# A two-layer hybrid decoder in one program: x's first tile on ScalarE's queue, and the score products of two differential heads issued as one block

## The chip, the cores and the metric

The kernel runs on one core of a Trainium2 chip. The metric is the device time of one execution in microseconds, the median of several runs. Five engines work side by side, each on a list of instructions of its own that it takes strictly in order: TensorE (PE in the profile), VectorE (DVE), ScalarE (ACT), GpSimd (POOL) and SyncE (SP, which here only starts DMAs). They wait for one another through semaphores.

## The reference

All of it is f32, with 256 tokens, a model width of 1024 and two layers. Cut to what matters here:

```python
for l in range(DEPTH):                                    # DEPTH = 2
    h = rms_norm(x, norm_mix[l])
    qkv = (h @ w_in[l]).reshape(B, S, 3, 16, 64)          # w_in: 1024 x 3072
    # heads 0..3: differential attention, two softmaxes of 32 dimensions each
    s1, s2 = q1 @ k1.T * scale, q2 @ k2.T * scale         # causal
    o_a = (softmax(s1) - lam * softmax(s2)) @ v
    # heads 4..9: three dilated windows mixed; heads 10..15: block-sparse, here plain causal
    x = x + concat(o_a, o_b, o_c) @ w_out[l]
    x = x + memory_cross_attention(rms_norm(x, norm_cross[l]), rms_norm(mem, norm_mem[l]), ...)
    x = x + (silu(g) * u) @ w_down[l]                     # g, u = rms_norm(x, norm_ffn[l]) @ w_gate_up[l]
```

## The kernel before

**Split products.** Every weight tile of 128 x 2048 numbers (a *unit*, 1 MB, loaded by SP into one of three ring slots `raw`, `whi`, `wlo`) is rounded by ACT (`split_hi`, line 591 or 583) into `whi`, and DVE (`split_lo`, line 886) writes the rest into `wlo`. PE then makes hi·hi, hi·lo and lo·hi. A slot is loaded again when both splits of the unit in it are done. x is treated in the same way: PE transposes a quarter of x (`build_x`, line 1394), ACT writes `thi` (`x_hi`, line 603), DVE `tlo` (`x_lo`, line 946).

**The sequence g.** The first stage of each layer is written by hand as steps g = 0, 1, 2, ... PE does one *filler* per step, four matmuls 128x512 of the q/k/v projection (line 1457, six steps to a unit, twelve to a chunk of 512 columns). Tables at the foot of the file say at which g the other work stands between the fillers, and ACT and DVE go through the same g in their own lists:

- `CHAIN_AT[e]`: DVE's norm of the k heads with its rotary (e = 0, 2) or of the q heads (e = 1, 3; the rotary of q is then POOL's, lines 534 to 537). `QKT_AT[e]`: PE's transposes of those heads (line 1548), and ACT's and DVE's copies of them to `kT`, `qT`.
- `S_AT[d]`: PE's `score(d)` (line 1587): the products of softmaxes 2d and 2d+1 with two query tiles, each f32 matmul standing in the trace as two records. There are 20 softmaxes: 0 to 7 are the eight of the four differential heads (32 rows of the array each), the rest have 64 rows. At the same g DVE does `mask_max` for both softmaxes (line 1117), which reads PSUM and writes `prob`. ACT's exponentials (`exps`, line 679) stand one and two steps later, and DVE's `combine` (lines 1126 to 1131: p1 - lam*p2 of a differential head) four steps later.
- `T_AT[m]`: PE transposes head m's probabilities (line 1599). `V_AT[m]`: PE's product with v (lines 1622 to 1624).
- DVE has, besides, `reduce_squares` (line 1024) at g = 12i + 13, and `split_lo` of unit g//6 + 2 at every g with g % 6 = 1. ACT has `split_hi` of that unit at g % 6 = 0, the copies of finished chunks (line 647) and the squares (line 657).

Two score blocks share two PSUM banks, so `score(d)` waits until DVE has read the block before (`nmax`). `mask_max` waits, where a `prob` buffer is used again, until PE has transposed the old one. The six tiny DVE steps of `lambdas` (line 984) run once, in layer 0.

## Time and profile before

| | us |
|---|---|
| median of 3 runs | 723.79 |
| lowest and highest of them | 720.84, 726.49 |
| the profiled execution | 718.44 |
| its span, first to last instruction | 716.6 |
| PE busy in the span | 693.4 |
| DVE busy | 474.6 |
| ACT busy | 396.7 |
| POOL busy | 128.4 |

The profile is of one execution, and its span lies 1.8 us below that execution's own time. The profile's page gives busy times, a chain of waits followed back from the end, and groups of instructions; the trace behind it gives each stretch in order of time, with a note in brackets where an engine sat idle and what released it. A row of the timeline merges neighbours: "x8" is eight records, and the duration is from the first's start to the last's end. Since neighbours overlap, the distance between two starts is the better price of a step.

### The profile page before, as it was taken

The numbers are of one execution on the slowest core, as the hardware profiler recorded it, in microseconds if no ns is written. First come the engines' busy times: TensorE is split into PE (matmuls) and PEld (weight loads), VectorE is DVE, ScalarE is ACT, GpSimd is POOL, SyncE is SP. The second block draws the span as 40 slices with busy tenths as digits, with TensorE's granted clock in tenths as the row PEclk, the third lists the DMA queues.
The fourth block names the chain that finished last, engine by engine and source line by source line (L and its number), as shares of the span: only waits on it lengthen the run. The fifth ranks groups of instructions, "written<-read, shape, count | busy, mean of one in ns | idle before, by whom it ended". The sixth has DMA issues, their size and how long they took to land.

```text
span 716.6 us, 10788 instructions
## 1 busy us (share of the span) xinstructions
PE 693.4 (97%) x3820; PEld 584.1 (82%) x3820; DVE 474.6 (66%) x935; ACT 396.7 (55%) x645; POOL 128.4 (18%) x100
## 2 busy tenths in 40 slices
PE   6999999999999999999999999999899999999997
PEld 4877788878988888888878878888688888888886
DVE  3899944374866666666569897344566666666665
ACT  5965767376644444444466658764765444444442
POOL 7131027507000000000031210662440000000000
PEclk9999999998999999999999999999999999999999
DMA  9945422244466666556545635022455566666631
GB/s 305 316 137 175 142 95 89 89 117 145 147 180 180 198 198 184 176 176 176 183 169 179 234 116 177 17 102 71 111 175 174 176 181 201 204 202 194 188 117 59
DMA packets 121215, 115.64 MB, mean 161 GB/s; under 512 B 3008, under 2 KB 95312, under 8 KB 121184
## 3 DMA queue, kind: packets, MB, share of 16 engines
q1 hardware_dynamic: 120224, 113.32, 50.8%
q0 software_dynamic: 384, 1.14, 0.6%
q10 hardware_dynamic: 576, 0.77, 0.3%
q8 instruction: 18, 0.29, 0.2%
q14 instruction: 13, 0.11, 0.0%
HBM read 114.17 MB, written 1.05 MB: 161 GB/s over the span
## 4 chain that ended last, share of the span: by engine, by line
PE 83%; DVE 11%; ACT 4%; issue 1%; DMA 1%; POOL 0%; SPq 0%; ACTq 0%; DVEq 0%
PE ps L1813 20%; PE ps L1457 16%; PE ps L1818 11%; PE ps L1850 5%; PE ps L1851 5%; PE ps L1852 5%; PE ps L1526 3%; DVE wlo L886 3%; PE ps L1835 3%; PE ps L1420 2%; PE ps L1587 2%; PE ps L1781 2%; PE ps L1394 2%; PE ps L1599 1%; ACT whi L591 1%; PE ps L1623 1%
## 5 line engine op out<-in xcount | busy, mean ns | idle before, releaser
L886 DVE TENSOR_TENSOR wlo<-raw,whi 128x2048 fp32r<-128x2048 f32 (+1 forms) x89 | 197.7, 2240 | 37.3 <-ACT whi L591 36.1
L591 ACT ACTIVATE whi<-raw 128x2048 fp32r<-128x2048 f32 (+1 forms) x103 | 191.0, 1878 | 14.3 <-PE ps L1852 7.3
L1813 PE MATMUL ps<-both,whi 128*128 128x512 f32 x640 | 159.2, 391 | 0.0
L1813 PEld LDWEIGHTS ps<-both,whi 128*128 128x128 f32 x640 | 117.6, 188 | 22.7
L1457 PE MATMUL ps<-whi,both 128*128 128x512 f32 x384 | 101.8, 401 | 2.7 <-ACT whi L583 2.0
L486 POOL TENSOR_TENSOR wlo<-raw,whi 128x2048 fp32r<-128x2048 f32 x15 | 68.5, 4581 | 196.3 <-DVE xs L975 180.8
L834 ACT ACTIVATE qkv<-ps 128x512 f32<-128x512 f32 x44 | 26.4, 599 | 126.9 <-PE ps L1818 121.7
L1818 PEld LDWEIGHTS ps<-both,wlo 128*128 128x128 f32 x640 | 87.3, 190 | 6.2
L1818 PE MATMUL ps<-both,wlo 128*128 128x256 f32 x640 | 89.2, 282 | 0.0
L1457 PEld LDWEIGHTS ps<-whi,both 128*128 128x128 f32 x384 | 71.4, 190 | 19.3 <-ACT both L603 2.4
L1850 PE MATMUL ps<-whi,ahi 128*128 128x512 f32 x176 | 69.3, 394 | 1.6 <-DVE alo L1353 1.6
L1851 PE MATMUL ps<-wlo,ahi 128*128 128x512 f32 x176 | 69.0, 392 | 0.0
L1852 PE MATMUL ps<-whi,alo 128*128 128x512 f32 x176 | 68.5, 389 | 0.0
L1332 DVE TENSOR_TENSOR qkv<-ps,qkv 128x512 f32<-128x512 f32 x44 | 30.3, 688 | 52.5 <-ACT qkv L834 52.4
L1457 PE MATMUL ps<-wlo,both 128*128 128x512 f32 x192 | 53.6, 401 | 0.1
L842 ACT ACTIVATE qkv<-qkv 128x256 f32<-128x256 f32 x44 | 18.4, 418 | 57.7 <-DVE qkv L1337 57.7
L679 ACT ACTIVATE sq<-sq,nm 128x128 f32<-128x128 f32 x80 | 35.4, 448 | 15.7 <-DVE nm L1117 15.5
L1457 PEld LDWEIGHTS ps<-wlo,both 128*128 128x128 f32 x192 | 34.7, 188 | 10.3 <-issue 3.3
L946 DVE SCALAR_TENSOR_TENSOR both<-ps,g_rows,both 128x128 fp32r<-128x128 f32 x96 | 25.9, 343 | 22.9 <-ACT both L603 22.9
L1850 PEld LDWEIGHTS ps<-whi,ahi 128*128 128x128 f32 x176 | 33.2, 189 | 8.2 <-DVE alo L1353 2.5
L1852 PEld LDWEIGHTS ps<-whi,alo 128*128 128x128 f32 x176 | 33.1, 188 | 7.2
L1851 PEld LDWEIGHTS ps<-wlo,ahi 128*128 128x128 f32 x176 | 33.2, 189 | 5.2
(202 smaller groups left out, 923.8 us busy)
## 6 DMA issues: line engine op xcount, KB each, us to landing
raw<-in_w_gate_up SPq DMA_DIRECT2D x88, 512.0 KB, 5.1
raw<-in_w_in SPq DMA_DIRECT2D x23, 1024.0 KB, 5.2
raw<-in_w_down SPq DMA_DIRECT2D x22, 1024.0 KB, 4.9
raw<-in_w_out SPq DMA_DIRECT2D x8, 1024.0 KB, 5.0
raw<-in_w_mkv SPq DMA_DIRECT2D x4, 1024.0 KB, 5.3
raw<-in_w_mq SPq DMA_DIRECT2D x4, 512.0 KB, 3.6
raw<-in_w_mo SPq DMA_DIRECT2D x2, 1024.0 KB, 4.9
xs<-in_x SPq DMA_DIRECT2D x2, 512.0 KB, 5.6
```

Source lines behind the costliest of these rows:

```text
L486: pool.tensor_tensor(wlo[s][:, 0:n], raw[s][:, 0:n], whi[s][:, 0:n].bitcast(F32), ALU.subtract)\
L591: ins = act.activation(whi[s][:, cols], raw[s][:, cols], ACT.Copy)
L679: ins = act.activation(prob[n % 4][:, a:b], prob[n % 4][:, a:b], ACT.Exp, bias=nm[:, n, t:t + 1], scale=-1.0, accum_out=zs[:, n, t:t + 1])
L834: act.activation(small_gu[b], gu_banks(b, 1), ACT.Copy).then_inc(small_out.sem, 1)
L886: ins = dve.tensor_tensor(wlo[s][:, cols], raw[s][:, cols], hi, ALU.subtract)
L1332: dve.tensor_tensor(gu[b], gu_banks(b, 0), small_gu[b], ALU.add).then_inc(gu_done.sem, 1)
L1457: ins = pe.matmul(ps[:, acc, :], x_part[:, k0 + k, t * P:(t + 1) * P], w_part[s][:, 512 * k:512 * k + 512], start=first and k == 0 and par ...
L1813: pe.matmul(ps[:, bank, :], whi[s][:, a:a + P], both[:, :, k, :], start=(k == 0), stop=False)
L1818: ins = pe.matmul(ps[:, bank, 0:256], wlo[s][:, a:a + P], thi[:, k, :], start=False, stop=(k == KC - 1))
L1850: pe.matmul(acc, ahi[b][:, tok], whi[s][:, a:a + 512], start=first, stop=False)
L1851: pe.matmul(acc, ahi[b][:, tok], wlo[s][:, a:a + 512], start=False, stop=False)
L1852: ins = pe.matmul(acc, alo[b][:, tok], whi[s][:, a:a + 512], start=False, stop=last)
```

## The change

Its parts, in the order of the diff:

1. **Start.** x's first tile is loaded by ACT's queue, ahead of its two small constants, and no longer stands between the identity and the first weights on SP's queue. The first unit's four pieces are rounded half by DVE (0 and 1) and half by ACT (2 and 3); ACT does its two between the first and the second quarter of x, and DVE takes `wlo` piece by piece. PE runs eight dummy products of a tile of ones ahead of everything and three after the first transposes (`WARM`).
2. **Score block.** The scores of heads 0 and 1 are issued as one block at g = 45 and those of heads 2 and 3 at g = 55. The four softmaxes stand in row groups 0, 32, 64 and 96 and write four banks (0, 1, 3, 4) where two banks served before. DVE does its four `mask_max` together. ACT's exponentials of the second head stand two steps behind the first's.
3. **Waits.** Banks 3 and 4 also serve `transpose_qk(2)` and the first products with v, so these now wait until all eight differential softmaxes are masked (`nmax` 8).
4. **Tables.** The positions of nearly all steps of the stage move.

```diff
             sp.dma_start(ident, consts["ident"]).then_inc(s_ident.sem, 16)
-            sp.dma_start(xs[:, 0, :], x_in[:, 0, :]).then_inc(s_x[0].sem, 16)
...
+            x_in = x.rearrange("b (t p) d -> p (b t) d", p=P)
+            act.dma_start(xs[:, 0, :], x_in[:, 0, :]).then_inc(s_x[0].sem, 16)
             act.dma_start(g_rows[:].rearrange("p l g k -> p (l g k)"), consts["g_rows"]).then_inc(s_rows.sem, 16)
             act.dma_start(freqs[:], consts["freqs"]).then_inc(s_freq.sem, 16)
...
-                    for k in range(4):
+                    for k in (2, 3):
                         cols = slice(512 * k, 512 * k + 512)
                         act.wait_ge(s_first[k].sem, 16)
                         ins = act.activation(whi[s][:, cols], raw[s][:, cols], ACT.Copy)
...
-                        split_hi(0, 0)
                         squares_of_x(0, 0, 0)
                     for q in (2 * t, 2 * t + 1):
                         x_hi(layer, X_MIX, q)
+                        if layer == q == 0:
+                            split_hi(0, 0)
...
-                            if g == S_AT[d] + b + 1:
+                            if g == exp_at(d) + b + 1:
                                 exps(2 * d + b)
...
                 if layer == 0:
-                    for q in range(2):
-                        x_lo(layer, X_MIX, q)
-                    split_lo(0, 0)
+                    for k in range(2):
+                        cols = slice(512 * k, 512 * k + 512)
+                        dve.wait_ge(s_first[k].sem, 16)
+                        dve.tensor_copy(whi[0][:, cols], raw[0][:, cols]).then_inc(first_hi_dve.sem, 1)
+                    x_lo(layer, X_MIX, 0)
+                    for k in range(4):
+                        cols = slice(512 * k, 512 * k + 512)
+                        if k < 2:
+                            dve.wait_ge(first_hi_dve.sem, k + 1)
+                        elif k == 2:
+                            dve.wait_ge(first_hi.sem, 1)
+                        else:
+                            dve.wait_ge(hi_done[0].sem, 1)
+                        ins = dve.tensor_tensor(wlo[0][:, cols], raw[0][:, cols], whi[0][:, cols].bitcast(F32), ALU.subtract)
+                    ins.then_inc(lo_done[0].sem, 1)
+                    x_lo(layer, X_MIX, 1)
...
-                        ins = dve.tensor_tensor_reduce(prob[n % 4][:, a:b], ps[:, n % 2, a:b], masks[:, kind, a:b],
+                        ins = dve.tensor_tensor_reduce(prob[n % 4][:, a:b], ps[:, score_bank(n), a:b], masks[:, kind, a:b],
...
-                        if d < DIFF and g == S_AT[d] + 4:
+                        if d < DIFF and g == exp_at(d) + 4:
                             combine(d)
...
+            def warm_up(n):
+
+                for _ in range(n):
+                    pe.matmul(ps[:, 7, 0:P], ones[:], ones[:], start=True, stop=True)
+
+            pe.wait_ge(s_ones.sem, 1)
+            warm_up(WARM[0])
             pe.wait_ge(s_ident.sem, 16)
             for layer in range(DEPTH):
 
                 for q in range(2):
                     build_x(layer, X_MIX, q)
+                if layer == 0:
+                    warm_up(WARM[1])
 
...
                     for b in range(2):
+                        if e == 2 and b == 0:
+                            pe.wait_ge(nmax.sem, nmax.at(layer, 4 if QKT_AT[2] < S_AT[2] else 2 * DIFF))
                         if e == 3 and b == 0:
...
                 def score(d):
 
-                    if d:
+                    together = (d, d + 1) if d < DIFF else (d,)
+                    if d == 2:
+
+                        pe.wait_ge(nmax.sem, nmax.at(layer, 4))
+                        pe.wait_ge(qkT_act.sem, qkT_act.at(layer, 3 if QKT_AT[2] < S_AT[2] else 2))
+                        pe.wait_ge(qkT_dve.sem, qkT_dve.at(layer, 3 if QKT_AT[2] < S_AT[2] else 2))
+                    elif d:
                         pe.wait_ge(nmax.sem, nmax.at(layer, 2 * d))
                     for qa, qb, kb, a in ((0, P, P, 0), (P, 2 * P, 2 * P, P)):
-                        for n in (2 * d, 2 * d + 1):
+                        for n in range(2 * d, 2 * d + 2 * len(together)):
                             h, base, rows = SOFTMAXES[n]
                             q, k = qT[base:base + rows, h // 2, qa:qb], kT[base:base + rows, h // 2, 0:kb]
-                            ins = pe.matmul(ps[:, n % 2, a:a + kb], q, k, start=True, stop=True)
-                    ins.then_inc(scores.sem, 1)
+                            ins = pe.matmul(ps[:, score_bank(n), a:a + kb], q, k, start=True, stop=True)
+                            if a and n % 2:
+                                ins.then_inc(scores.sem, 1)
 
                 def transpose_p(m):
                     n = 2 * m if m < DIFF else m + DIFF
...
                     if m == 0:
 
+                        pe.wait_ge(nmax.sem, nmax.at(layer, 2 * DIFF))
...
-                    for d in range(DUOS):
+                    for d in (0, 2) + tuple(range(DIFF, DUOS)):
                         if g == S_AT[d]:
...
+WARM = (8, 3)
 QK_CHUNKS = (0, 1, 2, 3)
 
 
-CHAIN_AT = (14, 26, 46, 53)
-QKT_AT = (30, 43, 56, 72)
-S_AT = (45, 49, 55, 61, 67, 70, 73, 78, 83, 86)
-T_AT = (54, 57, 64, 69, 71, 72, 76, 77, 78, 79, 82, 83, 87, 88, 91, 92)
-V_AT = (64, 67, 69, 71, 77, 77, 78, 79, 82, 82, 86, 88, 91, 92, 95, 95)
+CHAIN_AT = (17, 31, 54, 60)
+QKT_AT = (32, 42, 60, 72)
+S_AT = (45, 45, 55, 55, 67, 70, 73, 78, 83, 86)
+T_AT = (52, 54, 64, 66, 71, 72, 73, 77, 78, 79, 82, 83, 87, 88, 91, 92)
+V_AT = (64, 67, 71, 73, 77, 77, 78, 79, 82, 82, 86, 88, 91, 92, 95, 95)
 V_CHUNKS = (4, 5)
 SUMS = [(0, 0, 0), (0, 0, 1), (1, 0, 0), (1, 0, 1), (1, 1, 0), (2, 0, 0), (2, 0, 1), (2, 1, 0)]
-SUB_AT = 75
+SUB_AT = 76
 MEM_AT = (19, 20, 21, 22)
-MEM_SQ_AT = 22
+MEM_SQ_AT = 21
 HB_AT = (81, 82, 91)
-KM_AT = 89
+KM_AT = 86
 N_BUILD = 3
-LAM_AT = 13
-MEM_ROOT_AT = 41
+LAM_AT = 7
+MEM_ROOT_AT = 42
 LAST = max(FILLERS + 3 * len(OUT1_EARLY) - 1, V_AT[-1])
 
 
...
+def exp_at(d):
+
+    return S_AT[d] + (2 * (d % 2) if d < DIFF else 0)
+
+
+def score_bank(n):
+
+    return (0, 1, 3, 4)[n % 4] if n < 2 * DIFF else n % 2
 
```

What the tables make of the lists, at the three places that matter most. PE in layer 0, before, from the first score block (line 1587, `kT` and `qT`) to the first transposes of probabilities (line 1599, `sq` holds `prob`):

```order
L1587 MATMUL ps<-kT,qT 128x128 x2
L1587 MATMUL ps<-kT,qT 128x256 x2
L1457 MATMUL ps<-whi,both 128x512 x4
L1457 MATMUL ps<-wlo,both 128x512 x4
L1457 MATMUL ps<-whi,both 128x512 x8
L1587 MATMUL ps<-kT,qT 128x128 x2
L1587 MATMUL ps<-kT,qT 128x256 x2
L1457 MATMUL ps<-wlo,both 128x512 x4
L1457 MATMUL ps<-whi,both 128x512 x8
L1457 MATMUL ps<-wlo,both 128x512 x4
L1457 MATMUL ps<-whi,both 128x512 x4
L1599 MATMUL ps<-ident_sb,sq 128x128 x3
```

Of the change (its lines are numbered higher: 1622 is the score block, 1635 the transposes of probabilities, 1577 those of the k heads), from the first transposes of probabilities on:

```order
L1635 MATMUL ps<-ident_sb,sq 128x128 x3
L1484 MATMUL ps<-wlo,both 128x512 x4
L1484 MATMUL ps<-whi,both 128x512 x4
L1635 MATMUL ps<-ident_sb,sq 128x128 x3
L1484 MATMUL ps<-whi,both 128x512 x4
L1622 MATMUL ps<-kT,qT 128x128 x4
L1622 MATMUL ps<-kT,qT 128x256 x4
L1484 MATMUL ps<-wlo,both 128x512 x4
L1484 MATMUL ps<-whi,both 128x512 x8
L1484 MATMUL ps<-wlo,both 128x512 x4
L1484 MATMUL ps<-whi,both 128x512 x4
L1577 MATMUL ps<-ident_sb,qkv 128x128 x8
```

The second head's probabilities are transposed two fillers behind the first's, the block of heads 2 and 3 follows one filler later, and the transposes of the k heads of the second half come five fillers after that; four blocks have become two.

DVE in the same stretch, before: the first two masks (line 1117), then the norm of the second half of k (from line 918 to 1085), then `combine(0)` (1126), two masks, `reduce_squares`, `split_lo` of unit 10 (886) and `combine(1)`.

```order
L1117 ISA nm 128x1
L918 TENSOR_SCALAR nv<-g 128x16
...
L1085 TENSOR_TENSOR qkv<-rope_dve 128x2x6x8
L1126 RECIPROCAL lam_z<-zs 128x2
...
L1131 SCALAR_TENSOR_TENSOR sq<-sq,lam_z 128x256
L1117 ISA sq,nm<-ps,table,q_root 128x128
...
L1024 TENSOR_REDUCE g<-sqc 128x2x8
L886 TENSOR_TENSOR wlo<-raw,whi 128x2048
L1126 RECIPROCAL lam_z<-zs 128x2
```

DVE now, from the last of the first four masks (line 1133) on: 1142 to 1147 is `combine`, 1040 the reduction, 889 `split_lo`, 921 to 1101 the norm of k.

```order
L1133 ISA nm 128x1
L1142 RECIPROCAL lam_z<-zs 128x2
...
L1147 SCALAR_TENSOR_TENSOR sq<-sq,lam_z 128x256
L1040 TENSOR_REDUCE g<-sqc 128x2x8
L889 TENSOR_TENSOR wlo<-raw,whi 128x2048
L1142 RECIPROCAL lam_z<-zs 128x2
...
L1147 SCALAR_TENSOR_TENSOR sq<-sq,lam_z 128x256
L921 TENSOR_SCALAR nv<-g 128x16
...
L1101 TENSOR_TENSOR qkv<-rope_dve 128x2x6x8
L1133 ISA sq,nm<-ps,table,q_root 128x128
```

Both combines and a `split_lo` now stand ahead of the norm of k, and four masks stand right behind it, ahead of everything that PE takes from DVE next.

ACT in the same stretch, before, from the last exponential (679) of softmax 1 on: a finished chunk (647), the squares (657), `split_hi` of unit 10 (591, slot 1), and only then softmax 2:

```order
L679 ACTIVATE sq,zs<-sq,nm 128x256
L647 ACTIVATE qkv<-ps,rs 128x512
L657 ACTIVATE sqc<-qkv 128x1024
L591 ACTIVATE whi1<-raw1 128x2048
L679 ACTIVATE sq,zs<-sq,nm 128x128
```

And now, from the finished chunk (650) on; 682 is softmax 2's exponential, in two parts, 660 the squares, 593 `split_hi`:

```order
L650 ACTIVATE qkv<-ps,rs 128x512
L682 ACTIVATE sq,zs<-sq,nm 128x128
L682 ACTIVATE sq,zs<-sq,nm 128x256
L660 ACTIVATE sqc<-qkv 128x1024
L593 ACTIVATE whi1<-raw1 128x2048
```

Softmax 2 has moved ahead of the squares and of that `split_hi`; softmax 3 still comes behind them.

## Rows read from the trace of the kernel before

**Rows 1.** The page's first part: busy us, share of the span, instructions.

```profile
PE 693.4 (97%) x3820; PEld 584.1 (82%) x3820; DVE 474.6 (66%) x935; ACT 396.7 (55%) x645; POOL 128.4 (18%) x100
```

**Rows 2.** Chain of waits over the first 60 us, summed by line.

```profile
by line: DVE wlo L886 25.9%; PE ps L1457 6.9%; ACT both L603 6.8%; ACT whi L591 6.0%; DMA xs<-in_x 6.0%; DVE g L1024 5.8%; DVE mlo L953 4.1%; issue 3.6%; PE ps L1394 3.3%; ACT L754 2.1%; ACT qkv L647 2.1%; ACT sqc L657 1.8%; ACT sq L618 1.3
```

**Rows 3.** Timeline of PE at the start: start, duration, instruction, idle before.

```profile
4.91 1.94 PE L1394 MATMUL ps<-ident_sb,xs 128*128 128x128 f32 x8 [4.91 <-DMA xs<-in_x]
...
8.87 4.13 PE L1457 MATMUL ps<-whi,both 128*128 128x512 f32 x8 [2.02 <-ACT whi L583]
```

**Rows 4.** Timeline of ACT and DVE around 28 us, layer 0.

```profile
27.12 1.90 ACT L591 ACTIVATE whi<-raw 128x2048 fp32r<-128x2048 f32 x1
27.25 1.22 DVE L1024 TENSOR_REDUCE g<-sqc 128x32 f32<-128x1024 f32 x1 [1.94 <-ACT sqc L657]
...
29.84 2.26 DVE L886 TENSOR_TENSOR wlo<-raw,whi 128x2048 fp32r<-128x2048 f32 x1
```

**Rows 5.** Timeline of DVE from the first masks on, layer 0.

```profile
59.74 0.34 DVE L1117 CUSTOM_DVE_ANT_0 sq<-ps,table,q_root 128x128 f32<-128x128 f32 x1
...
67.61 0.16 DVE L1126 RECIPROCAL lam_z<-zs 128x2 f32<-128x2 f32 x1
...
70.08 1.22 DVE L1024 TENSOR_REDUCE g<-sqc 128x16 f32<-128x1024 f32 x1
71.22 2.28 DVE L886 TENSOR_TENSOR wlo<-raw,whi 128x2048 fp32r<-128x2048 f32 x1
...
74.53 0.16 DVE L1039 TENSOR_SCALAR nv<-g 128x4 f32<-128x4 f32 x1
...
77.38 0.34 DVE L1117 CUSTOM_DVE_ANT_0 sq<-ps,table,q_root 128x128 f32<-128x128 f32 x1
...
81.60 0.16 DVE L1126 RECIPROCAL lam_z<-zs 128x2 f32<-128x2 f32 x1
```

**Rows 6.** Timeline of PE from the first score block on, layer 0.

```profile
58.66 0.92 PE L1587 MATMUL ps<-kT,qT 32*128 32x128 f32 x8
59.52 1.21 PE L1457 MATMUL ps<-whi,both 128*128 128x512 f32 x4
...
67.16 1.07 PE L1457 MATMUL ps<-wlo,both 128*128 128x512 f32 x4
...
68.98 0.49 PE L1599 MATMUL ps<-ident_sb,sq 128*128 128x128 f32 x3
69.22 1.17 PE L1457 MATMUL ps<-whi,both 128*128 128x512 f32 x4
...
74.67 0.55 PE L1599 MATMUL ps<-ident_sb,sq 128*128 128x128 f32 x3 [0.49 <-DVE sq L1131]
...
86.33 0.33 PE L1622 MATMUL ps<-qkv,probT 128*128 128x64 f32 x2
...
87.03 0.93 PE L1587 MATMUL ps<-kT,qT 64*128 64x128 f32 x8
```

**Rows 7.** Timeline of ACT after the first masks, layer 0.

```profile
60.53 0.40 ACT L679 ACTIVATE sq<-sq,nm 128x128 f32<-128x128 f32 x1 [1.07 <-DVE nm L1117]
...
62.61 0.69 ACT L647 ACTIVATE qkv<-ps,rs 128x512 f32<-128x512 f32 x1 [0.22 <-PE ps L1457]
...
64.30 1.90 ACT L591 ACTIVATE whi<-raw 128x2048 fp32r<-128x2048 f32 x1
```

**Rows 8.** Timeline of ACT and DVE ahead of layer 1's first masks.

```profile
408.02 0.58 ACT L665 ACTIVATE qT<-ps 128x512 f32<-128x512 f32 x1
...
410.73 0.34 DVE L1117 CUSTOM_DVE_ANT_0 sq<-ps,table,q_root 128x128 f32<-128x128 f32 x1
```

**Rows 9.** Timeline of POOL, the rotary of q, layer 0.

```profile
50.27 2.62 POOL L535 TENSOR_TENSOR rope_pool<-qkv,tab 128x128 f32<-128x128 f32 x1
```

**Rows 10.** Stretches: length, busy us (records) of each engine, PE clock, DMA.

```profile
155.00:162.00 7.00, 5.19 (x34) 3.53 (x34) 5.88 (x19) 4.52 (x13) 2.01 (x2) 0.91 0.34 83
162.00:170.00 8.00, 7.67 (x47) 7.27 (x45) 2.86 (x8) 6.33 (x12) 7.72 (x2) 0.65 0.22 66
```

More of the change, by code:

```diff
@@ L218, in trunk @@
         first_hi = signal("first_hi")
+        first_hi_dve = signal("first_hi_on_dve")
         s_first = [signal(f"first_weight_loaded{k}") for k in range(4)]
@@ L1452, in piece @@
                     for k in range(4):
-                        if first_piece and k < 3:
-                            pe.wait_ge(first_hi.sem, k + 1)
+                        if first_piece and k < 2:
+                            pe.wait_ge(first_hi_dve.sem, k + 1)
+                        elif first_piece and k == 2:
+                            pe.wait_ge(first_hi.sem, 1)
                         elif first_piece:
@@ L1857, in _ @@
                 gate_up(0, 0)
-                if layer == 0:
-                    pe.wait_ge(s_ones.sem, 1)
                 pe.wait_ge(diag_ready.sem, diag_ready.at(layer, 1))
```

## The prediction

> **What bounds the kernel now.** I read the page first: PE works 693.4 us of a span of 716.6 us [rows 1], so as a whole the program is bound by PE, and a gain has to shorten PE's list or fill one of its few gaps. The chain of waits over the first 60 us says something else about the stage that this change touches: its largest share, 25.9%, is DVE's `split_lo`, and PE's filler line has 6.9% [rows 2]. PE is busy there too, but it runs just behind DVE. DVE's timeline shows it: from 29.84 us [rows 4] to the first masks at 59.74 us and on to 81.6 us [rows 5] DVE's blocks follow one another nearly without a gap. And PE's timeline has the mark of it: at 74.67 us it has sat idle for 0.49 us for `combine(1)` [rows 6]. So I price the attention stage on DVE's list, and PE's only as the partner that may have to wait.
>
> **Prices.** Each is a distance between starts, in layer 0.
> - Filler: (68.98 - 67.16)/2 = 0.91 us. A transposition of probabilities: 0.24 us, and 0.1 us more on the filler behind it, 0.34 [rows 6].
> - Score block before: 59.52 - 58.66 = 0.86 us, and its next filler takes 0.14 more (1.21 against 1.07), so 1.0 us [rows 6].
> - One product with v: 87.03 - 86.33 = 0.70 [rows 6].
> - DVE: `combine` plus two masks is 70.08 - 67.61 = 2.47. Two masks plus the norm of k are 67.61 - 59.74 = 7.87. `reduce_squares` is 71.22 - 70.08 = 1.14. `split_lo` plus `combine` are 74.53 - 71.22 = 3.31, with `split_lo` at 2.20 (its 2.28 less the overlap), so `combine` is 1.11, two masks 1.36, the norm of k 6.51. The norm of q is 77.38 - 74.53 = 2.85. From 77.38 to 81.60 stand two masks, `split_lo` and the copy to `kT`: the copy is 0.66 [rows 5].
> - ACT: the first exponential starts 0.79 after the first mask. Two softmaxes take 62.61 - 0.22 - 60.53 = 1.86, so 0.93 each; chunk and squares 64.30 - 62.61 = 1.69; `split_hi` 1.90 [rows 7].
>
> **The score block.** Nothing in the trace has four row groups at work at once. If the four stand side by side, the joint block costs the old 1.0 us; if they only take turns in pairs, 2.0. The change removes two of four blocks in each layer, so PE's list gets shorter by between 0 and 4.0 us in both layers together. I take 4.0, since the old block puts eight records into 0.92 us [rows 6], which leaves no time for them one after another. [...] As the next parts show, this list is not what decides.
>
> **The start.** Now PE waits 4.91 us for x, and its first eight matmuls take 4.13 us [rows 3] where two groups of four take 1.82 later [rows 6]. Earlier work on PE and `whi` shared between two engines can give back at most that difference, some 2.3 us, and nothing at the least, since x now shares the DMA engines with the weights. I expect 1.3. But by 28 us DVE's and ACT's lists set the pace, and what they make of it counts. The lambda block, 29.84 - 27.25 - 1.14 = 1.45 us, moves to g = 7, into the 1.94 us in which DVE idles there [rows 4]. `split_lo` behind it cannot start at once: its `whi` is ready at 27.12 + 1.90 = 29.0 [rows 4], and ACT's list ahead of it gets a little longer in wait, so I place it at 29.4 for 29.84, 0.44 earlier. `lambda_ends` moves ahead too, some 0.4. So the first masks of layer 0 come about 0.9 us earlier than 59.74, at 58.9. The bounds are 0 and 1.9.
>
> **The first masks of layer 1.** There `split_hi` of unit 9 stood ahead of `qkT_out(1)` in ACT's list, and stands behind it now, both at g = 42. `qT` is copied at 408.02 [rows 8], now 0.91 earlier, and ends by 407.7. `whi` is ready at 409.6, `split_lo` takes 2.2, and the masks start at 411.8 for 410.73 [rows 8]: 1.1 us later, unless ACT has room elsewhere (bounds 0 and 1.5).
>
> **From the first masks to score block 4.** Call the start of the first mask M. Before, block 4 starts at 87.03 - 59.74 = M + 27.3 [rows 5, 6]. DVE's new list, in its order:
> - four masks to M + 2.7, `combine(0)` to 3.8;
> - the reduction needs ACT's squares. ACT does exponentials 0 and 1 to M + 2.65, the chunk to 3.4, exponential 2 to 4.3, squares to 5.25, `split_hi` 10 to 7.15, exponential 3 to 8.1. So the reduction runs 5.25 to 6.4;
> - `split_lo` 10 waits for its `whi`: 7.15 to 9.35. `combine(1)` to 10.45;
> - norm of k to 17.0, four masks to 19.7.
>
> PE reaches the transposition of head 1 with its scores, nine fillers and one transposition: 1.0 to 0.2 before M, plus 8.2 + 0.34, so M + 7.5 to 8.4. It waits for `combine(1)`, 2 to 3 us. From there it needs 0.34 + 0.91 + 1.0 + 4.55 = 6.8 to the transposes of k, M + 17.2. They wait for the rotary (17.0, there in time) and, new, for all eight masks: 19.7. A second wait of 2.5 us. This wait does not depend on the price of the block.
>
> Then DVE: `split_lo` 2.20, `combine(2)` 1.11, copy 0.66, norm of q 2.85, `combine(3)` 1.11, to M + 27.6. PE gets to head 3's transposition with 0.9 for the transposes of k, six fillers 5.46, 0.70 and 0.34, at M + 27.1: a third wait of 0.5. Behind it 0.24 + 1.0 + 0.70, and block 4 starts at M + 29.5. That is 2.2 later than before; 0.34 of it is head 3's transposition, which used to come later, so 1.9 per layer. What stands behind has slack: DVE waited for PE there.
>
> **The sum.** Layer 0: -0.9 + 1.9 = +1.0. Layer 1: +1.1 + 1.9 = +3.0. In all +4.0 us. The profiled execution of 718.44 becomes 722.4. The median of the runs shown, 723.79, lies 5.35 above that execution, and the same step on it gives 727.8 us, 0.6% more. The saved blocks (4.0 us of PE's list) and the start are in this sum, but PE spends them on waits: 5 to 6 us in each layer where it had 0.49.
>
> **Rivals.**
> - *The change does what it says, and PE stays the bound.* 4.0 from the blocks, 1.0 from the two old waits of 0.49, 2.0 from the start: 7.0 less, 716.8. For it: PE has 97% of the span. Against it: from `combine(1)` to the transposes of k DVE alone needs 6.51 + 2.72 = 9.2 us and PE 6.8, at prices that each stand in a row. It would need DVE to start that stretch 2.5 us ahead of PE. Something between this and the forecast (half of the waits) gives about 722. Chance 0.17, and 0.12 for the middle.
> - *POOL's rotary is caught.* In layer 0, `split_lo` of unit 7 now stands ahead of the norm of q, which then ends near 51.0, and POOL's four operations follow. One of them took 2.62 us [rows 9] while a `split_lo` ran beside it. If the last is caught by the next `split_lo`, the transposes of q wait 2.3 us and M moves by as much: 730.1. Against it: a reduction and a copy stand between, about 1.8 us. [...] Chance 0.10.
> - *The clock falls (slower).* [...] The two waits above leave PE idle for 5 of some 17 us. [...] Against it: around the old wait of 0.49 us the stage kept its full clock. Chance 0.13.
> - The forecast itself: 0.48.
>
> **How the numbers follow.** About 1%, 7 us, can be told from no change. Faster by more needs 716.5 or less: half of the first rival, 0.08. Slower by more needs 731.0: the clock, and a little of POOL's case, 0.14. Within 1%: 0.78. The forecast's own bounds are M's: 727.8 - 2.0 and 727.8 + 1.4. The range reaches to the first rival and towards the last, 717.5 to 731.5; outside lie most of the clock's case and a part of the first rival's, 0.2.
>
> **What would show it.** In the profile after: PE idle for `combine` at the second head's transposition, 2 to 3 us, and for the last mask at the transposes of the second half of k, about 2.5 us, in both layers; a score block of eight softmax products at 1.0 us; first masks near 58.9 and, counted from the layer's first filler, 1.1 later in layer 1; PE's idle time up by some 8 us. The forecast is wrong if those waits are under 1 us, if M comes 2 us earlier than said (then PE finds DVE ahead), or if the score block costs 2 us. If PE's clock is below 1.0 between 60 and 90 us, the last rival has come.

## The result, and the profile after

The changed kernel takes 723.6 us (median), the kernel before 719.7 us in the runs beside it: a ratio of 1.0046, 95% interval 1.0023 to 1.0068. By that ratio it is 3.3 us slower (the two medians lie 3.9 apart), within 1%. The 723.79 us that the prediction starts from was the median of three runs; the 719.7 is that of twenty. The profiled executions have spans of 721.0 and 716.6 us, 4.4 apart. Part 1 of the page after, and the chain's line:

```profile
PE 695.6 (96%) x3842; PEld 586.2 (81%) x3842; DVE 479.4 (66%) x940; ACT 395.7 (55%) x643; POOL 128.7 (18%) x100
...
PE 78%; DVE 12%; ACT 5%; POOL 2%; issue 2%; DMA 1%; ACTq 0%; DVEq 0%; POOLq 0%
```

PE is busy for 2.2 us more than in [rows 1], with two score blocks fewer in each layer. In part that is the eleven dummy products (22 records more), in part a fallen clock, which the next rows show. PE's timeline after, layer 0 (L1622 is the score block, L1635 the transposition of probabilities, L1577 that of k, L1484 the filler):

```profile
58.82 0.94 PE L1622 MATMUL ps<-kT,qT 32*128 32x128 f32 x16
...
67.47 1.08 PE L1484 MATMUL ps<-whi,both 128*128 128x512 f32 x4
71.51 0.79 PE L1635 MATMUL ps<-ident_sb,sq 128*128 128x128 f32 x3 [2.95 <-DVE sq L1147]
71.94 2.05 PE L1484 MATMUL ps<-whi,both 128*128 128x512 f32 x4
73.93 1.47 PE L1622 MATMUL ps<-kT,qT 32*128 32x128 f32 x16
...
80.04 1.03 PE L1577 MATMUL ps<-ident_sb,qkv 128*128 128x128 f32 x8
...
87.83 0.55 PE L1635 MATMUL ps<-ident_sb,sq 128*128 128x128 f32 x3 [0.28 <-DVE sq L1147]
...
89.85 0.93 PE L1622 MATMUL ps<-kT,qT 64*128 64x128 f32 x8
```

The sixteen records of the joint block (eight products) now take 0.94 us, as the eight of an old block did (0.92, [rows 6]). But the wait for `combine(1)` is 2.95 us for 0.49, and behind it a filler takes 2.05 for 1.08: the clock has fallen. The second wait of the forecast, 2.5 us at the transposes of k, is not there at all. The stretches of after (length, busy us of PE, PEld, DVE, ACT, POOL, then PE's granted clock, DMA share, GB/s):

```profile
60.00:67.00 7.00, 7.00 (x33) 5.73 (x32) 5.74 (x22) 5.14 (x15) 0.80 (x2) 1.00 0.77 252
67.00:72.00 5.00, 2.05 (x11) 1.44 (x9) 4.28 (x10) 2.17 (x6) 1.11 (x3) 0.97 0.02 7
72.00:76.00 4.00, 4.00 (x25) 2.59 (x24) 3.52 (x15) 2.29 (x2) 0.00 (x0) 0.61 0.71 254
76.00:90.00 14.00, 13.72 (x75) 11.32 (x75) 13.45 (x49) 10.03 (x28) 1.24 (x4) 1.00 0.24 77
150.00:180.00 30.00, 25.98 (x180) 21.99 (x179) 18.21 (x47) 20.64 (x52) 15.66 (x5) 1.00 0.50 141
```

PE was busy for 2.05 of 5 us, then the granted clock was 0.61 on the mean for 4 us (0.50 in each microsecond from 72 to 75), then 1.00 again. Layer 1 has the same behind its wait of 2.27 us (0.57 from 423 to 427 us, 0.50 from 424 to 426). At 160 us, where the clock had fallen before [rows 10], it stayed full.

DVE's timeline after, layer 0, M being the first mask:

```profile
61.06 0.34 DVE L1133 CUSTOM_DVE_ANT_0 sq<-ps,table,q_root 128x128 f32<-128x128 f32 x1
...
66.16 1.22 DVE L1040 TENSOR_REDUCE g<-sqc 128x16 f32<-128x1024 f32 x1 [1.19 <-ACT sqc L660]
67.96 2.38 DVE L889 TENSOR_TENSOR wlo<-raw,whi 128x2048 fp32r<-128x2048 f32 x1 [0.59 <-ACT whi L593]
...
71.37 0.17 DVE L921 TENSOR_SCALAR nv<-g 128x16 f32<-128x16 f32 x1
...
76.80 0.35 DVE L1133 CUSTOM_DVE_ANT_0 sq<-ps,table,q_root 128x128 f32<-128x128 f32 x1
```

M is 61.06, not 58.9. From there the list runs much as forecast: reduction at M + 5.1 (5.25), `split_lo` at M + 6.9 (7.15), norm of k at M + 10.3 (10.45), second masks at M + 15.7 (17.0). In brackets are the forecast's places.

**Where the 4.4 us are.** Both traces are cut at three points: PE's transposes of x for the cross attention of layer 0 (143.10 before, 145.63 after), those that open layer 1 (363.75, 364.80), and those for its cross attention (494.06, 496.85). The four pieces differ by +2.53, -1.48, +1.74 and +1.61. The first splits at M: +1.32 ahead of it, +1.21 behind. The third too: +0.50 and +1.24. The second and the fourth hold no changed work. They differ, as far as the windows show, by where the clock fell: at 160 us only before, in the fourth piece only after (a mean of 0.94 from 520 to 550 us). A second profile of the kernel before (e8 below), with full clock in both, has 219.2 and 222.6 us for them, where before has 220.7 and 222.5 and after 219.2 and 224.2. The two nearly cancel.

### The profile page after: what moved, and what is told of

Read it like the earlier page. It is cut to its first block, busy times and chain, and to the rows that moved or that the text cites. A ratio compares the mean times of both kernels' runs of the same rounds, so it can differ in the third digit from the quotient of the medians.

```text
span 721.0 us, 10838 instructions
## 1 busy us (share of the span) xinstructions
PE 695.6 (96%) x3842; PEld 586.2 (81%) x3842; DVE 479.4 (66%) x940; ACT 395.7 (55%) x643; POOL 128.7 (18%) x100
## 3 DMA queue, kind: packets, MB, share of 16 engines
HBM read 114.17 MB, written 1.05 MB: 160 GB/s over the span
## 4 chain that ended last, share of the span: by engine, by line
PE 78%; DVE 12%; ACT 5%; POOL 2%; issue 2%; DMA 1%; ACTq 0%; DVEq 0%; POOLq 0%
PE ps L1850 20%; PE ps L1484 13%; PE ps L1855 11%; PE ps L1887 5%; PE ps L1888 5%; PE ps L1889 5%; DVE wlo L889 3%; PE ps L1553 3%; PE ps L1872 3%; ACT whi L593 2%; PE ps L1818 2%; PE ps L1436 2%; PE ps L1622 1%; PE ps L1635 1%; PE ps L1410 1%
## 5 line engine op out<-in xcount | busy, mean ns | idle before, releaser
L889 DVE TENSOR_TENSOR wlo<-raw,whi 128x2048 fp32r<-128x2048 f32 (+1 forms) x88 | 195.5, 2242 | 39.7 <-ACT whi L593 39.5
L1484 PE MATMUL ps<-whi,both 128*128 128x512 f32 x384 | 103.1, 405 | 2.6 <-ACT both L605 1.5
L1484 PEld LDWEIGHTS ps<-whi,both 128*128 128x128 f32 x384 | 72.0, 192 | 19.5 <-ACT whi L585 2.0
L1484 PE MATMUL ps<-wlo,both 128*128 128x512 f32 x192 | 53.2, 399 | 0.1
L1484 PEld LDWEIGHTS ps<-wlo,both 128*128 128x128 f32 x192 | 35.1, 189 | 9.6 <-issue 2.4
```

The source lines that it names most:

```text
L889: ins = dve.tensor_tensor(wlo[s][:, cols], raw[s][:, cols], hi, ALU.subtract)
L1484: ins = pe.matmul(ps[:, acc, :], x_part[:, k0 + k, t * P:(t + 1) * P], w_part[s][:, 512 * k:512 * k + 512], start=first and k == 0 and par ...
```

## Experiments

All ratios are against the kernel before on the same chip. M to block 4 is the distance from the first mask to score block 4; the layer's rest is from M to PE's transposes for the cross attention, layer 1.

| kernel | ratio (95%) | M to block 4, layers 0 / 1 | layer 1: opening to M | layer 1's rest |
|---|---|---|---|---|
| before | 1 | 27.29 / 27.26 | 46.98 | 83.33 |
| e8 before again | one execution | 27.09 / 27.06 | 46.97 | 83.13 |
| changed | 1.0046 (1.0023, 1.0068) | 28.79 / 28.79 | 47.48 | 84.57 |
| e1 start only | 1.0013 (0.9982, 1.0043) | 27.29 / 27.27 | 46.98 | 83.34 |
| e2 scores only | 1.0040 (1.0011, 1.0068) | 28.82 / 28.81 | 47.47 | 84.53 |
| e3 x on SP | 1.0040 (1.0007, 1.0073) | 28.80 / 28.80 | 47.47 | 84.46 |
| e4 head 1's transposition later | 1.0069 (1.0032, 1.0107) | 29.57 / 29.65 | 47.46 | 85.37 |
| e5 head 3's transposition later | 1.0043 (1.0017, 1.0069) | 27.81 / 27.63 | 47.46 | 83.67 |
| e6 transposes of k later | 1.0266 (1.0221, 1.0311) | 33.33 / 32.87 | 47.47 | 89.69 |
| e7 joint blocks on the old start | 1.0273 (1.0236, 1.0310) | 34.04 / 34.35 | 46.96 | 90.39 |
| e9 order mended | 0.9997 (0.9972, 1.0022) | 26.28 / 26.64 | 46.96 | 83.41 |
| e10 score products twice | 1.0051 (1.0023, 1.0079) | 28.90 / 29.21 | 47.54 | 84.99 |
| e11 less split_lo | 1.0009 (0.9985, 1.0033) | 27.38 / 27.42 | 47.45 | 83.19 |
| e12 no matmuls on ones | 1.0031 (1.0003, 1.0060) | 28.79 / 28.78 | 47.48 | 84.50 |

Where two profiles hold the same order (before and e8; changed, e3 and e12), the stage's lengths agree to 0.2 us, so they tell more than the whole times, which move by 0.3% either way.

### e1 and e2: the two halves of the change

e1 is the kernel before with the start part alone, e2 the changed kernel with that part undone.

> The kernel before with the start part alone: x's first tile on ScalarE's queue, the first weight tile converted half by DVE and half by ACT, the matmuls on ones ahead of x. The tables and the score blocks are those of before. Theory A (the start gives nothing, since x and g_rows land later and with them everything that ACT and POOL do up to 30 us): PE's filler of g = 12 starts at 24.3 us where before had 24.05, DVE's squares are reduced near 29 for 27.25, and the first masks of layer 0 stand 0.5 to 1.5 us later than 59.74, since DVE's list runs without a gap from there. The whole is 0 to +1.5 us. Theory B (the start gains as meant, and the changed tables ate it): g = 12 starts near 22.8, the first masks are 0.9 us earlier, the whole is 1 to 2 us less.

> The changed kernel with the start part undone: x on SP's queue, the first weight tile as before, no matmuls on ones; joint score blocks and all tables as changed. Theory A (the loss is in the attention stage: one wait of PE and the half clock behind it): the first masks of layer 0 stand near 59.7 for 61.06, PE still waits 2 to 3 us at the second probability transposition of each layer, with a stretch of half clock behind it, and score block 4 is 2.0 to 2.8 us later behind the first masks' block than before; the whole is +2 to +4 us against before, within 1 us of the changed kernel. Theory B (the start's late landings cost the time): within 0.5 us of before.

e1 leaves the attention stage as it was to 0.02 us, and e2 has all of the changed kernel's loss in it. For the stage, theory A of e2 holds: **the loss is in the joint blocks and their tables, not in the start.** The first masks of e1 came at 61.11 and its ratio is 1.0013, as its theory A said; but the kernel before has them at 61.13 in a second profile (e8), so this shows no loss by the start. On M e2 missed: 61.53, not 59.7. Its start came 0.7 later than that of the first profile of before, and its lists from there to M took 37.9 us for 36.8, where the changed kernel has 37.1. The last 0.8 stand in DVE's rows ahead of 41 us: a wait of 0.53 at 38.06, ahead of the rotary of k, and an operation of 0.50 for 0.22 at 39.66, beside POOL's rotary. What released the wait, the trace doesn't tell.

### e8, e3, e12: what the start part is worth

e3 moves one line back to SP's queue, e12 sets `WARM`:

```diff
+            sp.dma_start(xs[:, 0, :], x_in[:, 0, :]).then_inc(s_x[0].sem, 16)
...
-            act.dma_start(xs[:, 0, :], x_in[:, 0, :]).then_inc(s_x[0].sem, 16)
...
-WARM = (8, 3)
+WARM = (0, 0)
```

> The kernel before, unchanged, for a second profile of its start: it tells how far the landing of x and of the first weights moves from run to run. Theory A (start part gains nothing or loses): DVE's copy of rs starts at 22.9 to 23.7 us, earlier than in the runs with the new start (23.4 to 24.3). Theory B (the spread of the landings is as large as the difference): it starts above 23.7.

> The changed kernel with one line moved back: x's first tile goes through SP's queue behind the identity, as before; the rest of the start part and the tables stay. Theory A (g_rows behind x on ScalarE's queue holds ACT's first conversion of x and DVE's whole list, and freqs behind it holds POOL's angles): ACT's table load starts before 6.1 us, the first conversion of x near 6.0 for 7.4, PE's filler of g = 12 near 23.3 for 24.3, the first masks about 1 us earlier than 61.06; the whole 0.5 to 1.5 us less than the changed kernel. Theory B (the weights' share of the DMA engines decides): no difference over 0.3 us in any of these.

> The changed kernel without the matmuls on ones ahead of and behind the first transposes. Theory A (the landing of the first weight tile sets the start, PE's clock there does not): the granted clock between 5 and 10 us is lower, but ACT still waits for parts 2 and 3 of the first weight tile until 9.5 to 11 us, DVE's copy of rs starts at 23 to 24.3 us as in all other profiles, and the whole is the same within 1 us. Theory B (the warm-up is what keeps the start from being a loss): that copy is 1 us or more later, above 24.5 us.

DVE's copy of `rs`, the factors of x's norm, closes the start. The kernel before gave 22.95 us in its first profile and this in the second; e11, with the new start, gave the earliest of all:

```profile
24.31 0.16 DVE L939 COPY rs<-ny 128x2 f32<-128x2 f32 x1
```

```profile
22.36 0.17 DVE L944 COPY rs<-ny 128x2 f32<-128x2 f32 x1 [0.62 <-POOL ny L496]
```

So one and the same program moves by 1.4 us here, and e8's theory B holds. Four profiles with the old start (22.95, 24.31, 23.66 in e2, 23.32 in e7) have a mean of 23.6, the eight with the whole new one (22.4 to 24.7; without e3 and e12) of 23.8. No gain can be seen, and no loss. What holds the new start is first of all a transfer. ACT in the changed kernel, and in e12:

```profile
6.14 1.28 ACT L605 ACT_TABLE_LOAD   x1 [6.14 <-DMA g_rows<-in_g_rows]
7.43 1.14 ACT L605 ACTIVATE both<-ps,g_rows 128x128 fp32r<-128x128 f32 x4
9.79 1.38 ACT L585 ACTIVATE whi<-raw 128x512 fp32r<-128x512 f32 x2 [1.22 <-DMA raw<-in_w_in]
```

```profile
10.91 1.15 ACT L585 ACTIVATE whi<-raw 128x512 fp32r<-128x512 f32 x2 [1.95 <-DMA raw<-in_w_in]
```

ACT waits for the third or the fourth part of the first weight tile in every profile with the new start. Its first conversion behind such a wait starts at 9.0 to 11.1 us, and the copy of `rs` follows 13.1 to 14.2 us later in all ten. Besides, the copy itself waits for POOL in some of them, in the changed kernel for 0.62 us: POOL's operation ahead of it takes 2.46 us there, beside a `split_lo`, for 0.72 before.

```profile
21.49 2.46 POOL L496 TENSOR_TENSOR ny<-nv,minus_half 128x2 f32<-128x2 f32 x1
```

With x back on SP's queue (e3) its table load is at 2.94 and its first conversion at 5.64 us, 1.8 earlier, and then it waits 3.22 us for that part, until 10.00. So the first links of e3's theory A came, but its end did not: `rs` at 23.77 for 23.98, M at 60.85 for 61.06, the ratio 1.0040 for 1.0046. For these theory B holds. Without the matmuls on ones (e12) the eight transposes of x take 1.94 us, as in the kernel before; with them they take 1.06 us in four profiles (e1, e3, e4, e10), 1.15 in e6 and 1.79 to 1.94 in the other four. The granted clock is 1.00 from 5 to 10 us in e12 too, so the lower one of its theory A is not there. Behind the transfer no difference shows: the stage is equal to 0.1 us and the ratio is 1.0031. `rs` at 24.57 lies just above the bound of 24.5 that theory B was given, but e9 and e10, which have the matmuls on ones, are at 24.68 and 24.63; so theory B is not shown either.

### e4: head 1's transposition later

```diff
-T_AT = (52, 54, 64, 66, 71, 72, 73, 77, 78, 79, 82, 83, 87, 88, 91, 92)
+T_AT = (52, 57, 64, 66, 71, 72, 73, 77, 78, 79, 82, 83, 87, 88, 91, 92)
```

> The changed kernel with one number changed: the transposition of head 1's probabilities at g = 57 for 54, so that three groups of matmuls and the score block stand ahead of it. Theory A (DVE's list sets the end of this stage; PE's wait only moves): no wait for combine(1) at the transposition, but 1.5 to 2.5 us at the transposes of k, which need all eight masks (79.5 us); block 4 starts at most 0.5 us earlier than 89.85; the whole within 1 us of the changed kernel. Theory B (the wait of 2.95 us and the half clock that follows it are the cost): the clock stays full between 60 and 90 us, block 4 is 2 to 3 us earlier, in both layers, and the whole is 3 to 5 us less, that is at or below the kernel before.

```profile
79.21 1.10 PE L1577 MATMUL ps<-ident_sb,qkv 128*128 128x128 f32 x8 [4.25 <-DVE nm L1133]
```

```profile
80.00:84.00 4.00, 4.00 (x14) 3.14 (x13) 3.79 (x13) 4.00 (x13) 0.00 (x0) 0.57 0.34 83
```

The wait is gone from `combine(1)` and stands, 4.25 us of it, at the transposes of k, for the last mask: theory A, and a price of the wait that I had set too low (1.5 to 2.5). The clock falls behind it again, and here nothing takes it in: block 4 is 0.8 later. PE reaches head 3's transposition at 88.15 us, 0.9 after `combine(3)` has ended (87.26), so it is PE that is late there.

```profile
86.41 0.85 DVE L1147 SCALAR_TENSOR_TENSOR sq<-sq,lam_z 128x128 f32<-128x128 f32 x2
```

```profile
88.15 0.49 PE L1635 MATMUL ps<-ident_sb,sq 128*128 128x128 f32 x3
```

No profile of this order with a full clock was taken, so the 0.8 is a reading of these rows. Theory A's "within 1 us of the changed kernel" was missed: the ratios, 1.0069 and 1.0046, lie 1.7 us apart, though their intervals overlap.

### e12 once more: the second wait, and what the fallen clock cost

e12 kept its full clock in both layers. PE there:

```profile
72.06 0.55 PE L1635 MATMUL ps<-ident_sb,sq 128*128 128x128 f32 x3 [2.90 <-DVE sq L1147]
...
80.29 1.06 PE L1577 MATMUL ps<-ident_sb,qkv 128*128 128x128 f32 x8 [1.11 <-DVE nm L1133]
...
88.40 0.55 PE L1635 MATMUL ps<-ident_sb,sq 128*128 128x128 f32 x3 [0.59 <-DVE sq L1147]
```

With M at 61.64 all three forecast waits are there, 4.6 us together. Block 4 is at M + 28.79, exactly as in the changed kernel, where the clock fell, the second wait is missing and the third is 0.28. **The fallen clock cost nothing in that stage: it took the place of waits for DVE.** Layer 1 says the same: M + 28.79 with the fall, 28.78 without.

e12 and e8 are a pair at full clock without dummy products, so their pages show the saved blocks by themselves, e12 first:

```profile
PE 687.3 (95%) x3820; PEld 580.0 (81%) x3820; DVE 479.2 (67%) x940; ACT 395.2 (55%) x643; POOL 125.1 (17%) x100
```

```profile
PE 691.4 (97%) x3820; PEld 581.8 (81%) x3820; DVE 474.3 (66%) x935; ACT 397.0 (55%) x645; POOL 128.7 (18%) x100
```

PE is busy for 4.1 us less, and idle for 7.8 us more (719.9 - 687.3 against 716.2 - 691.4). The forecast had 4.0 and "some 8". PE's list did get shorter, and the waits took more than that.

### e10 and e11: less PE, or less DVE

e10 makes the products of each joint block twice; in e11 `split_lo` of unit 10 covers 512 of 2048 columns (first and second piece of the diff).

```diff
-                        for n in range(2 * d, 2 * d + 2 * len(together)):
+                        for n in [n for _ in together for n in range(2 * d, 2 * d + 2 * len(together))]:
...
+                    if u == 10:
+                        cols = slice(0, 512)
```

> The changed kernel with the products of both joint score blocks made twice: each block costs PE 0.8 to 0.9 us more, 3.5 us in all four. Theory A (DVE decides, PE has that time to spare in its waits): the wait for combine(1) shrinks from 2.95 to about 2.1 us, block 4 of both layers starts within 0.3 us of where the changed kernel has it against the first masks, and the whole is the same within 1 us; then a cheaper block is worth nothing here either. Theory B (PE's list decides): block 4 is 0.9 to 1.7 us later in each layer and the whole is 2 to 3.5 us more.

> The changed kernel with DVE's split_lo of unit 10 cut to its first 512 of 2048 columns, in both layers: 1.65 us of DVE's work are left out between the first masks and combine(1), so a part of the weights' low half is stale. Theory A (DVE decides): combine(1) 1.3 us earlier (then it waits for its exponentials), PE's wait for it 1.6 for 2.95, the second masks at M + 14.4 for 15.7, block 4 1.3 us earlier than M + 28.8; the whole is 2 to 3 us less than the changed kernel. Theory B (PE decides): PE's wait shrinks, block 4 moves by less than 0.3 us and the whole not at all.

PE in e10, then DVE's shortened `split_lo` and PE in e11 (M = 59.74):

```profile
72.14 0.55 PE L1637 MATMUL ps<-ident_sb,sq 128*128 128x128 f32 x3 [2.32 <-DVE sq L1147]
```

```profile
66.63 0.77 DVE L891 TENSOR_TENSOR wlo<-raw,whi 128x512 fp32r<-128x512 f32 x1 [0.58 <-ACT whi L593]
```

```profile
68.77 0.55 PE L1637 MATMUL ps<-ident_sb,sq 128*128 128x128 f32 x3 [1.52 <-DVE sq L1149]
...
87.12 0.93 PE L1624 MATMUL ps<-kT,qT 64*128 64x128 f32 x8
```

Twice the products (the first block takes 1.52 us to the next filler for 0.87) move block 4 by 0.1 and 0.4 us and the ratio from 1.0046 to 1.0051. They come out of PE's waits: theory A. (Layer 1's 0.4 goes beyond its 0.3 by a little. It came in through ACT: DVE waits 1.59 us for the squares there, for 1.19 in e12.) DVE's 1.5 us less bring block 4 forward by 1.4 us in each layer and the ratio to 1.0009: theory A. **DVE's list decides this stage.** What the joint block saves PE in here is worth nothing. e11 computes a wrong low half of that weight tile and serves for its time alone.

### e5, e6, e7, e9: other orders

All four have the fourth number of `T_AT` at 69 for 66. e6 adds `QKT_AT` and `V_AT` as shown; e7 has these with 43 for 42, on the old start; e9 has 43 for 42 and 60 kept in `QKT_AT`, 64 kept and 68 for 67 in `V_AT`, and the last line.

```diff
-QKT_AT = (32, 42, 60, 72)
+QKT_AT = (32, 42, 63, 72)
-V_AT = (64, 67, 71, 73, 77, 77, 78, 79, 82, 82, 86, 88, 91, 92, 95, 95)
+V_AT = (66, 67, 71, 73, 77, 77, 78, 79, 82, 82, 86, 88, 91, 92, 95, 95)
...
-    return S_AT[d] + (2 * (d % 2) if d < DIFF else 0)
+    return S_AT[d] + (3 * (d % 2) if d < DIFF else 0)
```

> The changed kernel with one number changed: the transposition of head 3's probabilities at g = 69 for 66, so that it stands behind score block 4 as before the change. M is the start of the first mask. Theory A (DVE's list decides, and what holds block 4 is first the last of the eight masks at M + 18.5, then combine(3) at M + 26.6): without combine(3) ahead of it block 4 starts at M + 27.0 to 27.4 where the changed kernel has M + 28.8, in both layers; the wait of 2.95 us at head 1's transposition stays; the whole is 2 to 3.5 us less than the changed kernel, about the kernel before. Theory B (PE's own list is what block 4 waits for, combine(3) cost it 0.3): block 4 is 0.6 us earlier, the whole 1.2 us less.

> The changed kernel with three numbers changed: head 3's transposition at g = 69 as in the run beside it, the transposes of the second half of k at g = 63 for 60, the first product with v at 66 for 64. Theory A (the waits are a matter of the order that DVE and PE meet in, and PE's shorter list shows once they are out of its way): PE waits for combine(1) as before, 2 to 3 us, but not at the transposes of k; block 4 starts at M + 25.6, the whole is 5 to 7 us less than the changed kernel. Theory B (PE's wait only moves on): PE waits at the product with v or behind block 4 for what it no longer waits for, and the score block 5 or 6 starts where it did; the whole is at most 2 us less than the changed kernel.

> As the run beside it, and with the start part undone, the lambda block back at g = 13, the norms of the first half back at g = 14 and 26, the transposes of q at 43 for 42: the kernel before with joint score blocks and four places moved. Theory A: the first masks of layer 0 stand 36.8 us behind DVE's copy of rs as before (the changed kernel 37.1, the scores alone 37.9), those of layer 1 are 47.0 us behind the layer's first transposes (47.5), block 4 at M + 25.6 in both layers; the whole is 3 us less than the kernel before and beats both. Theory B: the same as the kernel before within 1 us, since DVE's list from M on is as long as it was.

> The changed kernel with head 3's transposition behind score block 4 (g = 69), the transposes of q at 43 for 42, the second product with v at 68 for 67 and the second pair of exponentials one place later, so that ACT makes the squares ahead of them. Theory A (DVE's list from the first masks M to the last of the eight is what counts, and 1.19 us of it is a wait for ACT's squares): that wait goes to 0.3 us, the second masks start at M + 15.0 for 15.7, those of layer 1 stand 47.0 us behind the layer's first transposes for 47.5, block 4 is at M + 26.2 for 28.8; the whole is 1 to 2 us less than the kernel before. Theory B (what ACT is made to do later, combine(1) waits for): no change of the second masks, block 4 at M + 27.

e5: block 4 is 1.0 and 1.2 us earlier, but the transposition that stood ahead of it now follows, and the layer's rest is shorter by 0.9; by its ratio, 1.0043, no gain shows. Its expectation was too high. e6 had the wait for `combine(1)` (2.94) and none at the transposes of k, as expected, but block 4 at M + 33.3, not 25.6, and was 2.7% slower. DVE and PE in e6:

```profile
88.95 0.74 DVE L1116 TENSOR_SCALAR kT<-ps,k_col 128x512 f32<-128x512 f32 x1
```

```profile
89.95 0.41 PE L1659 MATMUL ps<-qkv,probT 128*128 128x64 f32 x2 [2.49 <-DVE kT L1116]
```

At g = 63 the copy to `kT` stands in DVE's list behind the norm of q, `combine(3)` and `split_lo` 12: 88.95 us where the changed kernel has 82.82. PE's first product with v needs its banks. e7 (ratio 1.0273) has the same, with a wait of 5.32, so it says nothing on joint blocks with the old start; only its M came nearly as expected (37.0 behind `rs`, 46.96 in layer 1). A place in the table is a place on two engines, and I had looked at PE's only.

e9, PE and DVE:

```profile
71.71 0.55 PE L1635 MATMUL ps<-ident_sb,sq 128*128 128x128 f32 x3 [1.98 <-DVE sq L1147]
...
88.29 0.93 PE L1622 MATMUL ps<-kT,qT 64*128 64x128 f32 x8
```

```profile
66.36 1.22 DVE L1040 TENSOR_REDUCE g<-sqc 128x16 f32<-128x1024 f32 x1 [0.46 <-ACT sqc L660]
```

Its steps came as expected: ACT's squares ahead of two exponentials shorten DVE's wait from 1.19 to 0.46, the second masks start at M + 15.0, layer 1's M is back at 46.96. The end did not: block 4 is early (M + 26.3 and 26.6), but head 3's transposition and a product with v now stand behind it, and the layer's rest is 83.41, that of before. e9 equals the kernel before (0.9997) and does not beat it.

## Why the prediction was right or wrong

**In short.** The mechanism was right: DVE's list holds PE up behind the joint blocks. The steps that failed are terms of the sum. The start and the lambda block were to bring M of layer 0 forward by 0.9 us and set it back by 0.3; M of layer 1 was to come 1.1 later and came 0.5 later; and the norm of k, taken at 6.51 us from the old order, took 5.43 in the new one. By the forecast's own signs, too, the second wait, "under 1 us", counts against it: it is 0 in the changed kernel, where the fallen clock took its place, and 1.1 in e12. The stated median failed by its base besides (see "The sum").

**The score block: right.** I took 1.0 us with the next filler; it is 0.94 for 16 records, 0.87 to the filler's start and 0.14 on it. Going from two row groups to four cost nothing for these products of 128 and 256 columns: 0.94 us for twice the records of the old 0.92.

**That this list does not decide: right**, shown from both sides by e10 and e11.

**The start: wrong, and M of layer 0 with it.** Two steps failed. The first is "I expect 1.3": PE's late start (4.91 us) and its slow first products (4.13 us for 1.82, at a granted clock of 1.00) were real, but in the new order ACT waits for the last parts of the first weight tile until 9.0 to 11.1 us. I had named the shared DMA engines as the reason for the lower bound 0 (their busy share in the changed kernel is 1.04 and 1.08 in the two microseconds from 4 to 6, and x lands at 5.3), and no gain beyond the spread of the starts was measured; why the parts land when they do, no run shows. The second is the lambda block "into the 1.94 us in which DVE idles". DVE's part fits there. Its exponential on ACT moved too, and stands ahead of the squares that DVE idles for:

```profile
26.60 1.28 ACT L768 ACT_TABLE_LOAD   x1
27.90 0.20 ACT L768 ACTIVATE lam_exp<-lam_dot 128x4 f32<-128x4 f32 x1
...
28.71 1.06 ACT L660 ACTIVATE sqc<-qkv 128x1024 f32<-128x1024 f32 x1
```

Table load and exponential delay the squares by 1.4 to 1.5 us; before, they came behind the squares. Counted from the copy of `rs`, the reduction starts 5.90 us later (29.88) for 4.30 before, `split_lo` 7.63 for 6.89, M 37.08 for 36.79. So the lists lose 0.3 where I had them gain 0.9. (This is read from the traces; no run moves the lambda block alone. With the block at its old place and the new start, e1 has M 36.83 behind `rs`.) The other 1.03 of M's 1.32 is how far this profile's start came later, less than the 1.4 between two profiles of the kernel before. The same table load takes 1.28 us in the kernel before too, at 29.04; the figure was at hand, the place was what I missed.

**M of layer 1: right in cause, too large.** ACT and DVE ahead of it:

```profile
408.12 1.91 ACT L593 ACTIVATE whi<-raw 128x2048 fp32r<-128x2048 f32 x1
```

```profile
410.07 2.29 DVE L889 TENSOR_TENSOR wlo<-raw,whi 128x2048 fp32r<-128x2048 f32 x1 [1.31 <-ACT whi L593]
412.28 0.34 DVE L1133 CUSTOM_DVE_ANT_0 sq<-ps,table,q_root 128x128 f32<-128x128 f32 x1
```

`split_hi` behind `qkT_out(1)` makes DVE wait 1.31 us, as said. The layer opens 1.05 later, so M is 0.50 late for 1.1: ACT's copy of `qT` ended 0.6 before the bound that I used. e9, with 43 back in the table, gets the 0.5 back.

**From M to block 4: the three waits are right, their size not.** At block 4 the forecast was +2.2, measured +1.50 and +1.53; net of head 3's transposition it was +1.9 per layer, measured +1.21 and +1.24 over the layer's rest. The term that was mis-sized is the norm of k, 6.51 us. After, it takes 76.80 - 71.37 = 5.43. The instructions are the same, and all of the difference lies in its first four rotary operations (64.80 to 66.61 before, 75.07 to 75.80 after). The first rotary pair of before, with POOL's beside it, then of after:

```profile
64.80 0.44 DVE L1082 TENSOR_TENSOR rope_dve<-qkv,tab 128x64 f32<-128x64 f32 x1
65.16 0.64 DVE L1083 TENSOR_TENSOR rope_dve<-qkv,tab 128x64 f32<-128x64 f32 x1
```

```profile
64.47 0.69 POOL L534 TENSOR_TENSOR rope_pool<-qkv,tab 128x192 f32<-128x192 f32 x1 [7.70 <-ACT sqc L657]
65.11 0.60 POOL L535 TENSOR_TENSOR rope_pool<-qkv,tab 128x192 f32<-128x192 f32 x1
```

```profile
75.07 0.23 DVE L1098 TENSOR_TENSOR rope_dve<-qkv,tab 128x64 f32<-128x64 f32 x1
75.21 0.22 DVE L1099 TENSOR_TENSOR rope_dve<-qkv,tab 128x64 f32<-128x64 f32 x1
```

My price was read where POOL's rotary ran beside DVE's; in the new order POOL's runs beside a reduction and the wait. That POOL is the cause was not tested by a run of its own; it rests on the rows, in both layers. So the masks end at M + 18.45 for 19.7, and the second wait is 1.1 us (e12) for 2.5. A part comes back at `combine(3)`, which now has POOL's last rotary beside it: 87.69 - 86.33 = 1.36 us for the 1.11 of the forecast.

**The rivals.** PE as the bound: refuted by e10 and e11. POOL caught: its last operation is what the transposes of q wait for, 0.37 us, but no `split_lo` caught it. The clock: it fell once in the stage of each layer, as the rival's name says, but I had put 2.8 us on a fall. That was worked out from the 8 us at 0.65 in [rows 10], where the trace of before grants 0.50 in each microsecond from 161 to 167: (1 - 0.65)/0.5 x 8 = 5.6 us at 0.50, half of them lost (an estimate). The fall in the changed kernel was shorter, 4 us at 0.61 with 0.50 from 72 to 75, in the same way 3.1 us at 0.50. A filler there takes 2.05 us for 1.08, so about half of that, 1.6 us, was lost (an estimate). It was covered by the waits, since PE was ahead of DVE anyway: block 4 is at M + 28.79 with the fall and without (e12). In this stage only e4 shows a fall that costs.

**The sum.** Forecast +1.0 and +3.0, together +4.0; in the profiles +2.53 and +1.74, together +4.3, or 3.2 without the 1.03 of the start's spread, against 3.3 measured. That the total came close is luck: errors of opposite sign met, layer 0's M was 1.2 us too early, layer 1's M 0.6 and each stage about 0.7 too late. The median of 727.8 us was 4.2 above the measured 723.6, and nearly all of it is the base: 723.79 from three runs, for 719.7.

## What to carry to other kernels

Where two engines run at nearly the same pace, a saving on one is worth what the other's list leaves of it: double the saved work once and cut the other engine's once, and the two numbers say who decides. When an entry of an order table moves, move it in thought on every engine that reads the table, for what it is now ahead of as well as behind. A price taken from a trace holds for its neighbours too: look at what ran beside it before carrying it to another place.

## What the hardware showed that I had not expected

- DVE's small two-input operations took longer where POOL's elementwise work ran beside them: 0.44 and 0.64 us for 0.23 and 0.22, some 1.1 us over one norm of k, in both layers. The reduction beside POOL's rotary at 66.16 was not slowed: 1.22 us, as before where no POOL operation ran beside it ([rows 5]). I had reckoned with longer operations for POOL only (its 2.62 us in [rows 9]).
- A wait of PE of 2.95 us is followed by about 4 us with a mean granted clock of 0.61 in the changed kernel, and by no fall in e2 (2.95) and e12 (2.90), and a wait of 2.27 in layer 1 by a fall in the changed kernel (0.57) and by none in e12; the clock of the kernel before fell at 160 us in one profile (0.89 from 150 to 180 us) and not in the other (1.00 in e8). What decides between them these runs don't show.
- The first 24 us of one and the same program differ by 1.4 us between two profiles, with the landing of the first transfers (`rs` was copied at 22.95 and at 24.31; in the second profile ACT waits 0.84 us for a part of the first weight tile, until 9.78, and in the first it does not wait).
